# Second block of a transformer kernel: low parts of a lift at later attention steps, three turns of heads inside dense products, a gate's split between two decay steps

## The reference, cut to what matters

```
h = rmsnorm(x, norm_mix)
(a_x, a_b, a_c, d_q, d_k, d_v, i_q, i_k, i_w, g_q, g_f, g_i, g_g, m_q, gate_logits) = split_cols(h @ w_in)
y_a = a_b * causal_conv3(a_c * a_x, conv_w)
y_b = sparse attention of 8 heads; each row keeps its top 64 keys by an index score of (i_q, i_k, i_w)
log_f = logaddexp(log(lb), log1p(-lb) + log_sigmoid(g_f));  y_c = gated linear recurrence with decays log_f
y_m = softmax(rmsnorm(m_q) @ rmsnorm(m_k).T / sqrt(128)) @ m_v        # 4 heads of 128, memory of 256 tokens
merged = sum over n of sigmoid(gate_logits[n]) * (branch[n] @ w_lift[n])     # branches y_a, y_b, y_c, y_m
x = x + merged @ w_out;  x = x + (silu(gate) * up) @ ffn_w_down
```

## Time and profile before

| | us |
|---|---|
| median of 3 runs | 2446.37 (2444.81 to 2447.39) |
| the profiled execution's own time | 2446.54 |
| its span in the profile | 2444.8 |
| PE busy | 2380.5 (97% of the span) |
| DVE busy | 1629.9 (67%) |
| ACT busy | 1128.9 (46%) |
| second block | from about 1380 to the end of the span |

### The profile page before, as it was taken

The page is one execution under the profiler, slowest core; times in us unless marked ns, Lnnn a source line. Parts: engine busy times, 40 slices in busy tenths (PEclk is TensorE's granted clock), DMA queues, the critical chain, the costliest instruction groups (busy, mean ns, idle before and its releaser), DMA issues.

```text
span 2444.8 us, 33463 instructions
## 1 busy us (share of the span) xinstructions
PE 2380.5 (97%) x13600; PEld 2002.2 (82%) x13600; DVE 1629.9 (67%) x2282; ACT 1128.9 (46%) x1571; POOL 167.0 (7%) x182
## 2 busy tenths in 40 slices
PE   7999999999999999999999999999999989999999
PEld 5788887787888778887888878888888878888887
DVE  6766755547667576677776676777676666677664
ACT  3644344444443434436434355564443454574442
POOL 2100002021000320000100100000100000001000
PEclk9999999999999999999999999999999999999999
DMA  6365343343553445543654344344754434444652
GB/s 233 134 215 206 138 172 138 138 173 134 194 206 138 173 166 196 207 158 123 244 203 161 128 172 170 140 174 146 275 206 156 151 115 162 173 173 168 235 172 89
DMA packets 258776, 419.08 MB, mean 171 GB/s; under 512 B 11937, under 2 KB 149153, under 8 KB 258625
## 3 DMA queue, kind: packets, MB, share of 16 engines
q1 hardware_dynamic: 253760, 400.15, 46.4%
q0 software_dynamic: 4864, 16.80, 1.9%
HBM read 415.86 MB, written 1.05 MB: 171 GB/s over the span
## 4 chain that ended last, share of the span: by engine, by line
PE 88%; DVE 6%; ACT 3%; issue 2%; DMA 1%; POOL 1%; SPq 0%; DVEq 0%; ACTq 0%
PE bank_L L2343 19%; PE bank_L L2359 17%; PE bank_S L2688 7%; PE bank_T L2653 7%; PE bank_L L2653 7%; PE bank_O L2688 7%; PE bank_T L2658 4%; PE bank_L L2658 4%; PE bank_L L2340 4%; DVE wlo L1565 2%; PE bank_O L2343 1%; PE bank_O L2605 1%; PE bank_S L2343 1%; ACT whi L1188 1%; PE bank_T L2300 1%
## 5 line engine op out<-in xcount | busy, mean ns | idle before, releaser
L1565 DVE TENSOR_TENSOR wlo<-raw,whi 128x2048 fp32r<-128x2048 f32 x316 | 713.7, 2279 | 149.2 <-ACT whi L1188 148.8
L1188 ACT ACTIVATE whi<-raw 128x2048 fp32r<-128x2048 f32 (+1 forms) x294 | 549.3, 1894 | 51.4 <-DMA raw<-in_w_in 12.9
L2343 PE MATMUL bank_L<-whi,xt 128*128 128x512 f32 (+1 forms) x1600 | 494.0, 391 | 4.5 <-DVE wlo L1565 2.5
L2359 PE MATMUL bank_L<-whi,xt 128*128 128x512 f32 x1280 | 400.2, 394 | 6.9 <-DVE wlo L1565 5.2
L2343 PEld LDWEIGHTS bank_L<-whi,xt 128*128 128x128 f32 x1600 | 293.5, 189 | 64.0 <-issue 4.5
L2343 PE MATMUL bank_L<-wlo,xt 128*128 128x512 f32 (+1 forms) x800 | 309.0, 386 | 0.0
L2359 PEld LDWEIGHTS bank_L<-whi,xt 128*128 128x128 f32 x1280 | 237.9, 189 | 56.7 <-issue 7.3
L2359 PE MATMUL bank_L<-wlo,xt 128*128 128x512 f32 x640 | 250.5, 391 | 0.0
L1440 ACT ACTIVATE tok<-tok 128x256 f32<-128x256 f32 x96 | 40.1, 417 | 450.6 <-DVE tok L2059 450.6
L2653 PE MATMUL bank_T<-xt,whi 128*128 128x512 f32 x768 | 192.3, 392 | 0.0
L2653 PE MATMUL bank_L<-xt,whi 128*128 128x512 f32 x768 | 191.7, 392 | 0.0
(11 more groups left out here) (344 smaller groups left out, 3654.4 us busy)
## 6 DMA issues: line engine op xcount, KB each, us to landing
raw<-in_w_gate_up SPq DMA_DIRECT2D x176, 512.0 KB, 5.7
raw<-in_w_in SPq DMA_DIRECT2D x72, 1024.0 KB, 7.0
draw<-in_w_down SPq DMA_DIRECT2D x44, 1024.0 KB, 5.8
raw<-in_ffn_w_up SPq DMA_DIRECT2D x88, 512.0 KB, 5.6
raw<-in_b_w_qkv SPq DMA_DIRECT2D x36, 1024.0 KB, 7.0
draw<-in_ffn_w_down SPq DMA_DIRECT2D x22, 1024.0 KB, 5.9
raw<-in_w_lift SPq DMA_DIRECT2D x16, 1024.0 KB, 6.2
raw<-in_a_w_qkv SPq DMA_DIRECT2D x12, 1024.0 KB, 8.8
```

Source lines behind the costliest of these rows:

```text
L1188: act.activation(wide(whi, w, nkc, ncols)[:, ks, :], wide(raw, w, nkc, ncols)[:, ks, :], ACT.Copy) \
L1565: dve.tensor_tensor(wide(wlo, w, nkc, ncols)[:, ks, :], wide(raw, w, nkc, ncols)[:, ks, :], wide(whi, w, nkc, ncols)[:, ks, :].bitcast(F32 ...
L2343: mm = pe.matmul(banks[name][:, 0:st["ncols"]], xx[:, kk, t * P:(t + 1) * P], ww[:, kk, :], start=(kk == 0 and q == 0), stop=(kk == nkc - ...
L2359: mm = pe.matmul(banks[bank][:, :], xx[:, k, t * P:(t + 1) * P], ww[:, k, :], start=(k == 0 and q == 0), stop=(k == KC - 1 and q == 2))
```

## The change

1. `attention` takes a table `lows`, and the memory attention gets {4: first half, 5: second half} for VectorE's low parts of the lift's chunk, in place of steps 1 and 4. The fourth round of the top-k moves from step 5 to step 6.
2. `turn_within` makes a turn part of a product: TensorE does `turn_heads` ahead of the matmuls of step t = 1, k = 6 (two steps before the end), and ScalarE does `heads_hi` ahead of its evacuation of t = 1. It is used for `kd` in `gate(3, 0)`, for `mq` in `gate(3, 1)` and for `dq` in C_AX.
3. In the second layer's `decay_logs`, VectorE makes the low parts of the chunk of `gate(0, 1)` behind its first two operations and ahead of the four others; before, they came behind those four. ScalarE's order is as it was.

```diff
+        def turn_within(late, src, ready, dst, nb_=4, by=1.0):
+
+            st = turn(src, ready, dst, nb_, by)
+            st["kind"], late["within"] = "turn_within", st
...
-            turn(kd, kd_ok, kkT, 2)
+            turn_within(stages[-1], kd, kd_ok, kkT, 2)
...
-            turn(tc, q_ok, mqT, by=-128 ** -0.5)
+            turn_within(gate_st, tc, q_ok, mqT, by=-128 ** -0.5)
...
-            o_is = attention(units, [], (turn_done, n["turn"]), [], fill=[st], ps=ps2, rounds=(0, 2, 3, 5), left=2)
+            o_is = attention(units, [], (turn_done, n["turn"]), [], fill=[st], ps=ps2, rounds=(0, 2, 3, 6), left=2,
+                             lows={4: (n["w"], (0,)), 5: (n["w"], (1,))})
...
-            linear(lhs, w_cols(C_AX), NW, "act", turned=True, dst=blk(0).rearrange("p (h s) -> p h s", s=SEQ), after=[])
-            turn(tc, q_ok, dqT, by=BY)
+            st = linear(lhs, w_cols(C_AX), NW, "act", turned=True, dst=blk(0).rearrange("p (h s) -> p h s", s=SEQ), after=[])
+            turn_within(st, tc, q_ok, dqT, by=BY)
...
-            add("decay_logs", l=l, counts=counts, aev_z=n["aev"])
+            add("decay_logs", l=l, counts=counts, aev_z=n["aev"], w=n["w"] + 2)
...
+                        if st["within"]:
+                            heads_hi(st["within"])
                         evacuated(st, 1, LB[1])
...
+                    heads_hi(late["within"])
                     evacuated(late, 1, LB[1])
...
-                        if split_at(st["fill"], i, steps):
+                        if st["lows"] and i in st["lows"]:
+                            split_lo(*st["lows"][i])
+                        elif not st["lows"] and split_at(st["fill"], i, steps):
                             split_lo(*split_at(st["fill"], i, steps))
...
                     if k:
+                        split_upto(st["w"])
                         step.did(dve.tensor_tensor(headed(3), headed(3), by_channel[1], ALU.add))
...
+                    if st["within"] and t == 1 and k == nkc - 2:
+                        turn_heads(st["within"])
```

More of the change, by code:

```diff
@@ L292, in linear @@
             st = add("linear", lhs=lhs, ncols=ncols, nkc=nkc, turned=turned, evac=evac, w=n["w"], mid=mid, inside=inside,
-                     func=func, narrow=narrow, after=after, into=into, inside_at=inside_at, skip=0, c0=0, whole=ncols, **kw)
+                     func=func, narrow=narrow, after=after, into=into, inside_at=inside_at, skip=0, c0=0, whole=ncols,
+                     within=None, **kw)
             chunks.append((loads, nkc, ncols))
@@ L306, in half_linear @@
             st = add("linear", lhs=lhs, ncols=NW, nkc=4, turned=False, evac="lift", w=w, mid=None, inside=None, into=into,
-                     c0=half * NW, whole=D, half=half, **kw)
+                     c0=half * NW, whole=D, half=half, within=None, **kw)
             for t in range(T):
@@ L370, in headnorm, with attention @@
             return (rope_done, n["rope"])
-        def attention(units, ready, first, behind, lead=2, in_twos=False, fill=(), ps=sm, rounds=(), shared=False, left=0):
+        def attention(units, ready, first, behind, lead=2, in_twos=False, fill=(), ps=sm, rounds=(), shared=False, left=0, lows=None):
             add("attention", units=units, ready=ready, first=first, behind=behind, lead=lead, in_twos=in_twos,
-                fill=fill, ps=ps, qb=SB if fill else QB, rounds=rounds, left=left)
+                fill=fill, ps=ps, qb=SB if fill else QB, rounds=rounds, left=left, lows=lows)
             for st in behind:
```

## The result

The changed kernel takes 2431.22 us, median of 4 runs (2429.95 to 2433.91), against 2446.28 for the kernel before on the same chip (2444.81 to 2447.39). The ratio is 0.994, with a 95% interval of 0.9923 to 0.9957. The profiled execution took 2431.22 us with a span of 2429.5, so it stands on the median. 2430.3 had been predicted.

What follows compares the result with a forecast made beforehand. TensorE, busy for 97% of the span, was taken as the bound, so only its idle or slow-clock moments count. 2 × (5.66 + 1.00 + 0 + 0.65) + 1.49 = 16.1 us off 2446.37 gives 2430.3, range 2426.8 to 2437.

Steps and rivals of the forecast that it cites:

- Low halves at later steps: Memory attention: two TensorE gaps (2.32 and 1.66 us) and the slow clock go, 5.66 us a layer.
- The middle term: Memory attention, behind the first gap: 3.95 us at clock 0.57 return to full clock, 1.68 us a layer.
- the clock stays low whatever the gap: Rival, memory attention: the slow clock stays though the gap goes, 2433.7 us; chance 0.05.
- Turns of `mq`: Inside the gate's product: the memory attention's scores start 1.00 us earlier in each layer.
- Turns of `kd`: Before the select's scores: a 0.80 us wait goes but turns up as longer later waits; 0 gained.
- Turns of `dq`: Inside C_AX: sparse attention's scores come 1.01 us earlier, a later wait grows; 0.65 us a layer gained.
- Decay stage: Second layer, gate's low parts ahead of additions: 2.64 us gained, 1.15 given back at the next product; 1.49 net.
- came back at another unit: Rival, memory attention: the removed waits return at another unit, 2433.6 us or 2437.0 with the slow stretch; chance 0.13.
- the tail of the decay edit: Rival, second layer's decay stage: the tail takes more than the gate gains, turns bring nothing, 2435.1 us; chance 0.08.
- both shift along: After the lift and in feed-forward: VectorE's chain and the loads move with TensorE, so the gain lasts.
- no change: Rival: what is gained is waited for at the next transfer, giving 2446.4 us; chance 0.04.

Runs made afterwards that it cites:

- e2: The kernel before with only the lift's low halves and the fourth top-k round at their new steps; 2435.19 us, ratio 0.9955.
- e3: The changed kernel with the lift's first low half back at step 1, the second still at 5; 2435.56 us, ratio 0.9959.
- e4: The changed kernel with the lift's low halves at steps 3 and 4; 2435.12 us, ratio 0.9954.
- e1: The changed kernel with the lift's low halves back at steps 1 and 4 and the round at 5; 2441.13 us, ratio 0.998.
- e6: The kernel of e1 once more, one execution for its profile; 2442.42 us.
- e5: The kernel of e3 once more on another chip, one execution for its profile; 2441.2 us.
- e7: The changed kernel with the turns of `mq` and `dq` as stages of their own again; 2434.67 us, ratio 0.9952.
- e12: The changed kernel with the edits of e10 and e11, and the sparse attention's low halves at steps 2, 4, 7, 9; 2423.32 us, ratio 0.9903.
- e8: The changed kernel with the turn of `kd` as a stage of its own again, one execution; 2433.03 us.
- e11: The changed kernel with the gate chunk's high and low parts spread by halves between the select's relus and sums; 2426.53 us, ratio 0.9918.
- e9: The changed kernel with the gate's low parts behind the four decay additions again; 2433.65 us, ratio 0.9944.
- e10: The changed kernel with the decay stage's two low parts set ahead of and behind the operation releasing ScalarE's logarithm; 2429.59 us, ratio 0.9931.

## Why the prediction was right

**1. Low halves at later steps: 5.66 us a layer forecast, 5.7 measured.** Scores to lift went from 26.54 to 20.85 in e2 (26.51 to 20.87 in the second layer), against 20.9 forecast. The order on the measured durations was right about margins too. The two plain gaps are shown one by one: e3 has the first alone, 2.37 us a layer (2.32 forecast), and e4 the second alone, 1.70 (1.66). What is left of e2's 5.69 and 5.64 us is 1.62 and 1.57 for the clock. So the two gaps were worth 0.09 more than forecast and the clock about 0.1 less, and that the sum is met so closely is in part luck. The fourth round at step 6 in place of 5 was not tried by itself.

The middle term, 1.68 us of slow clock, has nearly the right size (1.51 to 1.62 measured) but a looser cause than I gave. The fall to mostly the 1.2 GHz level came behind the gap of 2.14 or 2.15 us in 8 of 10 cases: both layers of before, e1, e6 and e5, neither of e3. In the nine profiled kernels without that gap (after, e2, e4, e7 to e12) it came in none of 18, though e4 has a gap of 1.48 us at the later place. So in these traces the fall comes only behind this gap, and the gap does not always bring it. What decides between e3 and e5, one kernel with the same instructions ahead of the gap, stays open; time since the start alone doesn't, since the first layer's gap ended at 1460.12 in e3, without a fall, and at 1460.01 in e1 and 1460.13 in e6, with one. In the timed runs of e1 the mean clock was 0.998 or 0.999 in all nine, in those of e3 1.000 in three of four, and in the 27 runs of before beside the experiments 0.997 to 0.999, never the 1.000 that after has in three of four. So a fall is likely in most runs of before, which a mean over the whole execution can't show, while in some runs of e3 the 1.6 us a layer are not there to be lost. The Trainium skill ("TensorE: Matmul & The Clock Gate", section "Why this matters for your kernels") warns of longer gaps than this one; e3 agrees with it, and before, e1, e5 and e6 don't, and they decide: gaps shorter than those it names cost clock as well. The rival "the clock stays low whatever the gap" fell.

**2. Turns of `mq`: 1.00 forecast, 1.04 measured** (e7, first layer; 0.74 + 0.10 in the second, where the late transfer took part of it). The wait of 0.79 and the last turn's running out are gone.

**3. Turns of `kd`: 0 forecast, 0 measured.** A wait of 0.80 went and the waits behind it took over all of it. e8 shows that it is nothing in both layers, and e11 that splits standing in one lump ahead of relus and buffers are the reason.

**4. Turns of `dq`: 0.65 forecast, 0.53 measured** (54.91 to 54.38 from lift to values; 0.51 by e7). The scores came 0.91 us earlier (1.01 forecast). The table load, which follows the moved evacuation, came 0.15 earlier and not 0.3, and the first exponential 0.52 and not 0.65; so the wait at the values grew to 0.76.

**5. Decay stage: 1.49 forecast, 1.25 measured** (24.50 to 23.25; 1.27 by e9). The mechanism is the forecast one to the step: 2.64 gained at the gate (8.10 to 5.46), VectorE waiting 2.15 us (2.16 forecast) for the logarithm, and a wait of 1.30 us for the next low part, of which "about 1 us" had been said. What was off is the size of the give-back, 24.50 - 2.64 = 21.86 against 23.25, thus 1.39 and not 1.15. Of the 0.24, 0.16 is TensorE's arrival: it was taken from the piece of the chain that starts at 2166.20, while the first product of C_GI had begun at 2166.04. The rest is the low part, which moved 2.25 us (from +18.57 to +20.82) and not 2.16. That it is a give-back and can be had back is shown by e10.

**Sum.** The distances, in the order of the program (scores to lift in both layers, then the turns of `mq`, of `dq`, and the decay stage), add up to 5.78 + 5.75 + 0.96 + 0.62 + 0.53 × 2 + 1.25 = 15.4 us, with the memory scores 0.96 and 0.62 us nearer to the `mk` turns. Forecast were 16.1; the 0.7 between is 0.24 in term 4 over two layers, 0.24 in term 5, and 0.27 at the second layer's turns of `mq` (0.62 + 0.11 there), less 0.06 that the other terms brought above the forecast. From the first layer's `mk` turns to the end the profiled executions differ by 1025.57 - 1010.83 = 14.74. Of the 0.7 that this is below 15.4, 0.43 goes with the late transfer and 0.2 is lost behind C_GI (15.50 to 15.3), which I did not trace. The 0.56 us of the unedited part came on top by chance. None of the rivals took place as a whole: no wait came back at another unit, and the tail of the decay edit took about half of its gain. But "both shift along" was not quite so: the issues did, and one transfer still landed late enough to take 0.43 us, which is the rival "no change" on a small scale.

## What to carry to other kernels

In a queue that runs in order, put work whose input comes late behind the copies that a full engine waits for, and in halves: each half should stand where its input is made and where what stands behind it is not yet due. Before a wait is removed, look for the next thing in the same chain that ends later; if there is one, as for the `kd` turns, the edit is worth nothing until that is moved too. Where a moved piece stands ahead of the operation that releases another engine's long chain, move the release in front of it.

## What the runs showed of the hardware

- A gap of 2.14 or 2.15 us on TensorE was followed by a granted clock of 0.57 to 0.63 over the next 3.95 us in eight cases and by 1.00 in two, with the same instructions ahead; a fall costs 1.5 to 1.6 us. I had expected all or none.
- A gap of 1.48 us at the later place was followed by no fall in either layer of e4.
- Stretches inside one stage repeat to a few hundredths of a us across chips and executions where no transfer is waited for (20.75 or 20.76 from scores to lift in six kernels), while the start of the first layer's `mk` turns varies by 3.5 us; a change worth 1 us is to be read from the former.
